# The mLSTM key sums of one head taken tile by tile over batches 1 to 3

## The chip, the cores and the metric

The kernel runs on 1 core of one Trainium2 chip. The metric is the device time of one execution in microseconds (us). The kernel before takes 1183.11 us, the median of 3 runs (1175.84 to 1189.69).

## The reference, cut to what matters

The program is one inference step of two layers. Layer 0 mixes a gated recurrence with dilated attention; layer 1 is an mLSTM block with 4 heads of 512 dimensions. A prompt of 256 tokens and 8 sample sequences of 4 tokens each go through together, and all of it is in float32. The change touches the mLSTM block alone, and there the running sum of the keys, `n`:

```python
w_state = jnp.exp(bcum[:, -1:, :] - bcum + ic - m_new[:, None, :])
decay = jnp.exp(bcum[:, -1] + m - m_new)
kw = kc * w_state[..., None]
C_new = decay[..., None, None] * C + jnp.einsum('bshd,bshe->bhde', kw, vc)
n_new = decay[..., None] * n + jnp.sum(kw, axis=1)
```

For each head and each sequence there is a state matrix `C` (512 by 512) and a vector `n` (512). `C` gets the sum over tokens of outer products of weighted keys and values; `n` gets the sum over tokens of the weighted keys. The new `n` is only an output: nothing later in the step reads it. `C` before the update is read by the queries of the samples. The 8 samples bring their `C` from HBM and write it back (8 MB in and 8 MB out in every head's turn); the prompt starts from zero and writes its own.

## The kernel before, in words

Every engine has its own instruction stream, written out by hand, and semaphores order them. The dense projections multiply 128x128 weight tiles by 288 token columns in three products (high by high, low by high, high by low; lines 1964 to 1966). Between the projection into the mLSTM block and the one out of it lies the **state stage**, which is what matters here. It loops over 4 heads `h`, and in each over the 8 samples `b`, which the code calls batches.

In batch `b` TensorE does `old_state(h, b)` (the samples' queries times the old `C`, L2419, 4 products that use 32 columns of the array each) and `outer(h, b, 0)` and `outer(h, b, 1)` (the outer products of that sample, L2446, each half of `C` into two PSUM banks: banks 0 and 1, or 4 and 5, by turns). The prompt's own outer products are items of the same kind, `outer(h, NB, 0)` ahead of batch 3's and `outer(h, NB, 1)` ahead of batch 4's (L2449, 4 products of 512 columns). Each of them may begin when the item that last used its two banks has been taken out: VectorE does that for a sample (`new_state`, L1687, decay times old `C` plus the banks, into the ring `cring`), ScalarE for the prompt (`prompt_state`, L1090). SyncE stores each item when it is made (L637) and, when the store of an earlier item has freed a slot of the ring of ten, loads the item that comes eight later (L628). All of the stage's large transfers are on this one queue.

Other work of a head hangs on the batches. After batch 0 TensorE makes denominators and numerators of the prompt (L2375 to L2392). VectorE scales them into `hT` (L1751) and ScalarE squares `hT` (L1106). In batch 2 TensorE sums the squares over the rows, `row_squares` (L2457, 4 products of 256 columns against ones), ScalarE takes the root (L1108), VectorE the reciprocal (L1759) and two passes over `hT` (L1761 in batch 2, L1769 in batch 3). In batches 4 to 7 TensorE makes queries, keys and values of the next head.

The **key sums** are `key_sums`: for each of the 4 tiles `e` of a head's 512 dimensions, products of one column (the prompt's weighted keys, L2403) and one of eight columns (the samples', L2405), all into one PSUM bank. Before, they run in batch 1, two tiles ahead of `outer(h, 1, 0)` and two between it and `outer(h, 1, 1)`. VectorE's `new_n` (L1675 to L1678) turns them into the new `n` at the end of its batch 1.

Two PSUM banks, 6 and 7, are **staging banks**. Their users stand in the list `USES`, in the order of a head; use number `u` gets bank 6 + u % 2. Before TensorE writes use `u` it waits until use `u - 2`, the last one in that bank, has been read. `DVE_READS` names the uses that VectorE reads; `n` is one, `mean` (the row squares) is read by ScalarE. Every use counts up `stage_full` once, and its reader waits for its own number, so the order of the list must be the order in which TensorE finishes them.

Of the kernel before, what the change touches and what calls it, by code (L numbers as in the profile page):

```python
# [25 lines left out]
P = 128  # L26
D = 1024
SEQ = 256
NB = 8
# [21 lines left out]
NH = 4  # L51
DH = DC // NH
ET = DH // P
# [55 lines left out]
assert ITEMS % 2 == 0  # L109

USES = ["q0", "q1", "q2", "q3", "k0", "k1", "k2", "k3", "kt0", "kt1", "ks", "vt0", "vt1", "vs",
        "bc0", "bc1", "sc", "n", "mean"]
VT_BANKS = (6, 7, 2, 3, 6, 7)
AB_USES = (["qs", "q0", "ks", "k0"] + [f"r{m}" for m in range(4)] + [f"i{m}" for m in range(4)]
           + [f"r{m}" for m in range(4, 8)] + [f"i{m}" for m in range(4, 8)])
# [25 lines left out]
def program(nc, A, O):  # L141
    ctx = ExitStack()
    with ctx:
# [5 lines left out]
        def at(name, off, *dims, dt=F32, parts=P):  # L149

            off = (off + 31) // 32 * 32
            n = int(np.prod(dims))
            assert off + 4 * n <= ARENA, (name, off + 4 * n - ARENA)
            t = nc.alloc_sbuf_tensor_at(name, [parts, n], dt, offset=arena0 + off)[:, :]
            if len(dims) == 2:
                t = t.rearrange("p (a b) -> p a b", b=dims[1])
            if len(dims) == 3:
                t = t.rearrange("p (a b c) -> p a b c", b=dims[1], c=dims[2])
            return t, (off + 4 * n + 31) // 32 * 32
# [108 lines left out]
        seln, o = at("seln", o, NB, dt=F32R, parts=3 * NS)  # L268
        gsml, o = at("gsml", o, 2 + NB, parts=NH)
        tokg, o = at("tokg", o, 2, 2 * NH)  # L270
# [25 lines left out]
        ktok, o = at("ktok", o, 2, DH)  # L296
# [20 lines left out]
        kst, o = at("kst", o, 2, DH, dt=F32R, parts=3 * NS)  # L317
# [4 lines left out]
        ps = ctx.enter_context(nc.psum_tensor("ps", [P, 8, 512], F32))  # L322
# [179 lines left out]
        def use(h, name):  # L502

            return len(USES) * h + USES.index(name)
# [664 lines left out]
        def _(dve):  # L1169
# [574 lines left out]
            def chunk(h, b):  # L1744
                if b == 0:

                    dve.wait_ge(den_abs, h + 1)
                    order.after(dve.tensor_tensor(dn, dn, bc[:, h % 2, R_EN:R_EN + SEQ], ALU.max))
                    order.after(dve.reciprocal(dn, dn))
                    dve.wait_ge(num_psum, h + 1)  # L1750
                    dve.tensor_tensor(hT, ps[:, 4:6, :].rearrange("p a (c t) -> p (a c) t", t=SEQ),  # L1751
                                      dn.unsqueeze(1).to_broadcast([P, ET, SEQ]), ALU.mult).then_inc(h_ready, 1)
                    if h == 2:
                        sample_stats(0)
                if b == 1:
                    new_n(h)
                if b == 2:
                    dve.wait_ge(stage_read_a, reads(use(h, "mean"))[1])
                    order.after(dve.reciprocal(dn, dn))  # L1759
                    for e in range(ET):  # L1760
                        order.mark(dve.scalar_tensor_tensor(hT[:, e], hT[:, e], pcol("norm_w", ET * h + e), dn,  # L1761
                                                            ALU.mult, ALU.mult))
                    if h + 1 == NH:
                        dve_lo(0, 0, STEP0[OUT_C])
                if b == 3:
                    order.wait()
                    for e in range(ET):
                        m = ET * h + e
                        order.mark(dve.scalar_tensor_tensor(hT[:, e], xcc[:, m, 0:SEQ], pcol("skip", m), hT[:, e],  # L1769
                                                            ALU.mult, ALU.add))  # L1770
                    order.wait()
                    dve.wait_ge(z_ready, h + 1)
                    dve.tensor_tensor(hT, hT, z[:, ET * h:ET * h + ET, 0:SEQ], ALU.mult).then_inc(y1_full, 1)
                    if h >= 2:
                        sample_folds(h - 2)
                    if h == 2:
                        sample_gates(0)
                        sample_scales(0)
                    if h + 1 == NH:
                        dve_lo(1, 0, STEP0[OUT_C])  # L1780
                if b == 5 and h == 2:
                    sample_rows(0)
                if b == 5 and h + 1 < NH:
                    keys_low(h + 1)
                if b == 6 and h + 1 < NH:
                    values_low(h + 1)
                if b == 7 and h == 2:
                    sample_low(0)
                if b == (7 if h + 1 < NH else 4):
                    dve.wait_ge(y1_hi_ready, h + 1)  # L1790
                    dve.tensor_tensor(y1_lo[:, ET * h:ET * h + ET, 0:SEQ], hT, y1_hi[:, ET * h:ET * h + ET, 0:SEQ],
                                      ALU.subtract).then_inc(y1_ready, 1)
                if b == 7:
                    if h + 1 < NH:
                        queries(h + 1)
                        arguments(h + 1)
                        weights(h + 1)
# [153 lines left out]
        def _(pe):  # L1951
# [252 lines left out]
            for h in range(H):  # L2204
# [21 lines left out]
                for i in range(3):  # L2226
                    last = pe.transpose(ps[:, 6, P * i:P * i + P], pS[f][:, P * i:P * i + P], ident)
# [8 lines left out]
                out = ps[:, 7, SEQ * f:SEQ * f + SEQ]  # L2236
# [65 lines left out]
            def staged(h, name):  # L2302

                u = use(h, name)
                if u >= 2:
                    pe.wait_ge(*reads(u - 2))
                return ps[:, 6 + u % 2]
# [85 lines left out]
                                     skip_group_check=True)  # L2393
                last.then_inc(num_psum, 1)

            def key_sums(h, tiles):

                out = staged(h, "n") if 0 in tiles else ps[:, 6 + use(h, "n") % 2]
                for e in tiles:
                    c0 = (NB + 2) * e  # L2400
                    es = slice(P * e, P * e + P)
                    for tt in range(2):
                        pe.matmul(out[:, c0 + NB:c0 + NB + 1], ktok[:, tt, es], tokg[:, tt, NH + h:NH + h + 1],  # L2403
                                  start=tt == 0, stop=tt == 1)
                    last = pe.matmul(out[:, c0:c0 + NB], kst[:, h % 2, es], seln, start=True, stop=True)  # L2405
                if ET - 1 in tiles:
                    last.then_inc(stage_full, 1)

            def old_state(h, b):
# [98 lines left out]
            for h in range(NH):  # L2508
                for b in range(NB):
                    last = old_state(h, b)  # L2510
                    if b == NB - 1:
                        last.then_inc(hs_psum, 1)
                    if b == 1:
                        key_sums(h, (0, 1))
                    if b == 2:
                        row_squares(h)
                    if b in (3, 4):
                        outer(h, NB, b - 3)
                    outer(h, b, 0)
                    if b == 1:  # L2520
                        key_sums(h, (2, 3))
                    if h + 1 == NH and b + 1 == NB:
                        sum_groups(h)
                    outer(h, b, 1)
                    chunk(h, b)
# [145 lines left out]
```

## Time and profile before

| | us |
|---|---|
| median of 3 runs | 1183.11 |
| lowest and highest run | 1175.84, 1189.69 |
| the profiled execution, its device time | 1187.85 |
| the profiled execution, its span | 1185.9 |
| mean granted TensorE clock over the span | 0.966 |

All rows below are of this one profiled execution. Times in them are in microseconds from the start of its span. "Busy" of TensorE (PE) is the time in which a matmul is under way, whatever it does; PEld is its weight loads, which overlap. PEclk is the clock that TensorE was granted, as a share of its full 2.4 GHz; it has two levels, 1.00 and 0.50 (1.2 GHz), and a mean between them is a stretch with some of each. In a row of the timeline the first number is the start, the second the time from that start to the end of the group's last instruction; neighbouring matmuls overlap, so the time that a group takes from the engine is read from its start to the start of the next. Brackets at the end of a row give idle time ahead of it and what ended it.

### The profile page before, as it was taken

What the parts mean: (1) busy time and instruction counts of PE and PEld (TensorE: products, weight loads), DVE (VectorE), ACT (ScalarE), POOL (GpSimd) and SP (SyncE); (2) the same over time, 40 slices, a digit from 0 to 9 for tenths busy, and PEclk for the clock granted to TensorE, in tenths of its full rate; (3) what the DMA queues carried; (4) which work ended last, traced back from release to release, by engine and by line L of the source; (5) the groups of instructions that cost most, each with busy time, mean ns of one, the idle gap of its engine ahead of it and who ended that gap; (6) DMA issues with size and microseconds to landing.
All of it is one profiled execution on the core that took longest, in us unless ns stands there. A gap on an engine that the chain in (4) does not pass through costs nothing.

```text
span 1185.9 us, 21692 instructions
## 1 busy us (share of the span) xinstructions
PE 1101.5 (93%) x8497; PEld 962.3 (81%) x8497; DVE 660.9 (56%) x958; ACT 542.9 (46%) x884; POOL 150.4 (13%) x204
## 2 busy tenths in 40 slices
PE   4998998777999999999999999999998999999996
PEld 4986877656999999999899965656555999999995
DVE  4568674412456444343997636666768366544343
ACT  5332635212555554344475353645543366553431
POOL 5133000000002221001400220100000003220000
PEclk9998999788999999999999999898989999999998
DMA  9696897799334544454644039898989634554441
GB/s 339 220 345 251 309 347 283 264 327 381 129 122 148 169 163 160 164 172 160 232 143 143 19 107 337 318 358 282 386 298 404 215 107 165 169 167 160 163 140 40
DMA packets 92265, 260.97 MB, mean 220 GB/s; under 512 B 8837, under 2 KB 9861, under 8 KB 91801
## 3 DMA queue, kind: packets, MB, share of 16 engines
q1 hardware_dynamic: 91320, 257.92, 61.2%
q0 software_dynamic: 432, 1.29, 0.4%
q8 instruction: 56, 0.92, 0.3%
q10 hardware_dynamic: 432, 0.65, 0.2%
q14 instruction: 25, 0.20, 0.1%
HBM read 218.10 MB, written 41.73 MB: 219 GB/s over the span
## 4 chain that ended last, share of the span: by engine, by line
PE 80%; DVE 11%; ACT 4%; DMA 2%; issue 2%; POOL 0%; SPq 0%; POOLq 0%; ACTq 0%; DVEq 0%
PE ps L1964 19%; PE ps L1966 19%; PE ps L1965 19%; PE ps L2419 2%; PE ps L2446 2%; PE ps L2076 2%; DVE w_lo L1175 2%; PE ps L2157 2%; PE ps L2317 2%; PE ps L2449 1%; DMA kv_b<-in_kv 1%; PE ps L2457 1%; DVE rstd L1202 1%; PE ps L2324 1%; DVE cring L1687 1%
## 5 line engine op out<-in xcount | busy, mean ns | idle before, releaser
L1175 DVE TENSOR_TENSOR w_lo<-w_raw,w_hi 128x1024 fp32r<-128x1024 f32 x232 | 284.6, 1233 | 205.0 <-ACT w_hi L692 204.0
L692 ACT ACTIVATE w_hi<-w_raw 128x1024 fp32r<-128x1024 f32 x232 | 242.0, 1053 | 196.2 <-PE ps L1966 182.1
L1964 PE MATMUL ps<-xin_hi,w_hi 128*128 128x288 f32 x1016 | 308.3, 303 | 24.8 <-DVE w_lo L1175 23.7
L1965 PE MATMUL ps<-xin_lo,w_hi 128*128 128x288 f32 x1016 | 304.7, 300 | 0.0
L1966 PE MATMUL ps<-xin_hi,w_lo 128*128 128x288 f32 x1016 | 304.4, 300 | 0.0
L1964 PEld LDWEIGHTS ps<-xin_hi,w_hi 128*128 128x128 f32 x1016 | 194.8, 192 | 37.7 <-DVE w_lo L1175 21.1
L1965 PEld LDWEIGHTS ps<-xin_lo,w_hi 128*128 128x128 f32 x1016 | 194.3, 191 | 0.7 <-issue 0.2
L1966 PEld LDWEIGHTS ps<-xin_hi,w_lo 128*128 128x128 f32 x1016 | 193.8, 191 | 0.0
L1966 PE MATMUL ps<-hid_hi,w_lo 128*128 128x288 f32 x512 | 151.9, 297 | 0.0
L1965 PE MATMUL ps<-hid_lo,w_hi 128*128 128x288 f32 x512 | 151.4, 296 | 0.0
L1964 PE MATMUL ps<-hid_hi,w_hi 128*128 128x288 f32 x512 | 151.2, 295 | 0.0
L1687 DVE SCALAR_TENSOR_TENSOR cring<-cring,bc,ps 128x1024 f32<-128x1024 f32 x64 | 79.5, 1276 | 43.9 <-PE ps L2446 43.4
L1964 PEld LDWEIGHTS ps<-hid_hi,w_hi 128*128 128x128 f32 x512 | 96.7, 189 | 0.0
L1965 PEld LDWEIGHTS ps<-hid_lo,w_hi 128*128 128x128 f32 x512 | 96.3, 188 | 0.0
L1966 PEld LDWEIGHTS ps<-hid_hi,w_lo 128*128 128x128 f32 x512 | 96.1, 188 | 0.0
L1848 POOL TENSOR_TENSOR hid_lo<-relu,hid_hi 128x288 f32 x64 | 52.5, 820 | 181.5 <-ACT hid_hi L766 181.5
L1267 DVE SCALAR_TENSOR_TENSOR relu<-ps,rstd 128x288 f32<-128x288 f32 x64 | 29.1, 457 | 78.9 <-PE ps L1966 75.5
L764 ACT ACTIVATE relu<-relu 128x288 f32<-128x288 f32 x64 | 28.4, 443 | 69.9 <-DVE relu L1267 68.5
L1838 POOL COPY sqsum<-sq 128x288 f32<-128x288 f32 x5 | 3.1, 612 | 438.3 <-ACT sq L752 433.4
L2446 PE MATMUL ps<-vb,kst 96*128 96x512 f32 x128 | 46.4, 465 | 8.8 <-ACT cring L1090 5.2
L2446 PEld LDWEIGHTS ps<-vb,kst 96*128 96x128 f32 x128 | 22.5, 198 | 33.4 <-issue 14.7
L752 ACT ACTIVATE sq<-ps 128x288 f32<-128x288 f32 x32 | 13.2, 411 | 75.6 <-PE ps L1966 75.6
(398 smaller groups left out, 1710.8 us busy)
## 6 DMA issues: line engine op xcount, KB each, us to landing
w_raw<-in_weights SPq DMA_DIRECT2D x232, 512.0 KB, 3.3
cring<-in_C SPq DMA_DIRECT2D x64, 512.0 KB, 6.3
out_Cs<-cring SPq DMA_DIRECT2D x64, 512.0 KB, 6.2
kv_a<-in_kv SPq DMA_DIRECT2D x60, 448.0 KB, 5.7
kv_b<-in_kv SPq DMA_DIRECT2D x60, 448.0 KB, 5.8
out_Cp<-cring SPq DMA_DIRECT2D x8, 512.0 KB, 5.4
kv_w<-in_kv SPq DMA_DIRECT2D x8, 448.0 KB, 5.1
x<-in_x SPq DMA_DIRECT2D x1, 1152.0 KB, 7.5
```

What stands on the lines that cost most here:

```text
L692: act.activation(w_hi[:, l % UM], w_raw[:, l % W_SLOTS], ACT.Copy).then_inc(hi_ready, 1)
L764: act.activation(relu2[:, l % 2], relu[:, l % 2], ACT.Square).then_inc(relu2_ready, 1)
L1175: dve.tensor_tensor(w_lo[:, l % W_SLOTS], w_raw[:, l % W_SLOTS], w_hi[:, l % UM], ALU.subtract).then_inc(lo_ready, 1)
L1267: dve.scalar_tensor_tensor(relu[:, l % 2], ps[:, bank, 0:T], 0.0, rstd, ALU.max, ALU.mult).then_inc(out_taken, 1)
L1687: dve.scalar_tensor_tensor(cring[s], cring[s], bc[:, h % 2, R_DECAY + b:R_DECAY + b + 1], new, ALU.mult, ALU.add).then_inc(c_new, 1)
L1848: pool.tensor_tensor(hid_lo[:, bass.ds(m, 1)].rearrange("p a t -> p (a t)"), relu2[:, l], hid_hi[:, bass.ds(m, 1)].rearrange("p a t -> p ( ...
L1964: pe.matmul(out, w_hi[:, j, ws], hi, start=start and kk == 0, stop=False)
L1965: pe.matmul(out, w_hi[:, j, ws], lo, start=False, stop=False)
L1966: last = pe.matmul(out, w_lo[:, l % W_SLOTS, ws], hi, start=False, stop=stop and kk == UK - 1)
L2076: last = pe.matmul(ps[32 * b4:32 * b4 + 32, 4 + c, 0:NK // 2], qz_of[b4][:, h], kv[s][:, c * NK // 2:(c + 1) * NK // 2], start=h == 0, sto ...
L2157: last = pe.matmul(out, pT[:, kt, c0:c0 + 32], kv[s][:, P * kt:P * kt + P], start=kt == 0 and h % 4 == 0, stop=False, skip_group_check=True)
L2446: last = pe.matmul(out, kst[:, h % 2, es], vb[:, (NB * h + b) % 2], start=True, stop=True)
```

## The change

The key sums are taken one tile at a time: tile 0 ahead of `outer(h, 1, 0)` as before, tiles 1, 2 and 3 each between the two outer products of batches 1, 2 and 3. `row_squares`, in batch 2, now comes before the last two tiles, so `mean` changes places with `n` in `USES`. VectorE's `new_n` goes from batch 1 to batch 3, where it stands ahead of the pass L1769. The number and the shapes of all instructions stay as they are.

```diff
@@ -109,7 +109,7 @@
 USES = ["q0", "q1", "q2", "q3", "k0", "k1", "k2", "k3", "kt0", "kt1", "ks", "vt0", "vt1", "vs",
-        "bc0", "bc1", "sc", "n", "mean"]
+        "bc0", "bc1", "sc", "mean", "n"]
@@ -1752,7 +1752,7 @@
-                if b == 1:
+                if b == 3:
                     new_n(h)
                 if b == 2:
                     dve.wait_ge(stage_read_a, reads(use(h, "mean"))[1])
@@ -2393,17 +2393,16 @@
-            def key_sums(h, tiles):
-
-                out = staged(h, "n") if 0 in tiles else ps[:, 6 + use(h, "n") % 2]
-                for e in tiles:
-                    c0 = (NB + 2) * e
-                    es = slice(P * e, P * e + P)
-                    for tt in range(2):
-                        pe.matmul(out[:, c0 + NB:c0 + NB + 1], ktok[:, tt, es], tokg[:, tt, NH + h:NH + h + 1],
-                                  start=tt == 0, stop=tt == 1)
-                    last = pe.matmul(out[:, c0:c0 + NB], kst[:, h % 2, es], seln, start=True, stop=True)
-                if ET - 1 in tiles:
+            def key_sums(h, e):
+
+                out = ps[:, 6 + use(h, "n") % 2] if e else staged(h, "n")
+                c0 = (NB + 2) * e
+                es = slice(P * e, P * e + P)
+                for tt in range(2):
+                    pe.matmul(out[:, c0 + NB:c0 + NB + 1], ktok[:, tt, es], tokg[:, tt, NH + h:NH + h + 1],
+                              start=tt == 0, stop=tt == 1)
+                last = pe.matmul(out[:, c0:c0 + NB], kst[:, h % 2, es], seln, start=True, stop=True)
+                if e == ET - 1:
                     last.then_inc(stage_full, 1)
@@ -2511,14 +2510,14 @@
                     if b == 1:
-                        key_sums(h, (0, 1))
+                        key_sums(h, 0)
                     if b == 2:
                         row_squares(h)
                     if b in (3, 4):
                         outer(h, NB, b - 3)
                     outer(h, b, 0)
-                    if b == 1:
-                        key_sums(h, (2, 3))
+                    if 1 <= b < ET:
+                        key_sums(h, b)
                     if h + 1 == NH and b + 1 == NB:
                         sum_groups(h)
                     outer(h, b, 1)
```

## Rows read from the trace of the kernel before

**Rows 1.** The page: busy time of TensorE over the span, and its granted clock in 40 slices.

```profile
PE 1101.5 (93%) x8497; PEld 962.3 (81%) x8497; DVE 660.9 (56%) x958; ACT 542.9 (46%) x884; POOL 150.4 (13%) x204
PEclk9998999788999999999999999898989999999998
```

**Rows 2.** Busy time by stretch: the last head's turn in the state stage.

```profile
core 0: us, PE busy (x) PEld busy (x) DVE busy (x) ACT busy (x) POOL busy (x), PEclk, DMA share, GB/s
862.00:912.00 50.00, 45.58 (x235) 25.00 (x234) 38.02 (x58) 19.46 (x30) 0.00 (x0) 0.93 0.94 340
```

**Rows 3.** Busy time by stretch around the fall of the clock, heads 0, 1, 3; last, batch 5 of head 3.

```profile
709.00:713.00 4.00, 4.00 (x32) 2.91 (x24) 2.46 (x2) 1.06 (x1) 0.00 (x0) 1.00 0.55 207
713.40:716.70 3.30, 3.30 (x12) 1.50 (x5) 1.48 (x4) 1.90 (x2) 0.00 (x0) 0.50 0.87 225
764.60:771.30 6.70, 6.70 (x22) 3.77 (x21) 2.22 (x5) 2.00 (x2) 0.00 (x0) 0.50 0.74 256
873.90:880.50 6.60, 6.60 (x21) 3.66 (x20) 2.07 (x5) 2.00 (x2) 0.00 (x0) 0.50 0.78 239
896.00:899.00 3.00, 1.34 (x5) 0.60 (x4) 3.00 (x3) 0.39 (x1) 0.00 (x0) 1.00 1.06 409
```

**Rows 4.** The timeline of TensorE in batches 1 to 3 of head 0.

```profile
start us, us, engine line op out<-in xcount [idle before <-releaser]
709.77 0.61 PE L2403 MATMUL ps<-tokg,ktok 128*128 128x1 f32 x4
...
710.91 0.71 PE L2446 MATMUL ps<-vb,kst 96*128 96x512 f32 x2
711.45 0.50 PE L2403 MATMUL ps<-tokg,ktok 128*128 128x1 f32 x4
...
712.49 0.71 PE L2446 MATMUL ps<-vb,kst 96*128 96x512 f32 x2
713.13 1.81 PE L2419 MATMUL ps<-cring,qz 128*32 128x512 f32 x8
714.86 2.90 PE L2457 MATMUL ps<-qf,ones 128*128 128x256 f32 x8
717.41 1.28 PE L2446 MATMUL ps<-vb,kst 96*128 96x512 f32 x4
718.62 1.07 PE L2419 MATMUL ps<-cring,qz 128*32 128x512 f32 x8
719.62 3.70 PE L2449 MATMUL ps<-vw,ktok 128*128 128x512 f32 x8
722.75 1.03 PE L2446 MATMUL ps<-vb,kst 96*128 96x512 f32 x2
724.43 0.73 PE L2446 MATMUL ps<-vb,kst 96*128 96x512 f32 x2 [0.65 <-ACT cring L1090]
```

**Rows 5.** The timeline of TensorE in head 1, from the second outer product of batch 1.

```profile
764.94 1.20 PE L2446 MATMUL ps<-vb,kst 96*128 96x512 f32 x2
766.07 1.94 PE L2419 MATMUL ps<-cring,qz 128*32 128x512 f32 x8
767.94 3.66 PE L2457 MATMUL ps<-qf,ones 128*128 128x256 f32 x8
771.16 1.12 PE L2446 MATMUL ps<-vb,kst 96*128 96x512 f32 x3
```

**Rows 6.** The timeline of ScalarE, head 0: the prompt's first item taken out.

```profile
723.35 1.02 ACT L1090 ACTIVATE cring<-ps 128x1024 f32<-128x1024 f32 x1 [5.08 <-PE ps L2449]
```

**Rows 7.** The timeline of VectorE: `new_n` of head 0, then batch 2 of head 3.

```profile
714.43 0.16 DVE L1675 COPY pack_n<-ps 128x4 f32<-128x4 f32 x1
...
714.72 0.19 DVE L1678 TENSOR_TENSOR pack_n<-pack_n,ps 128x32 f32<-128x32 f32 x1
...
881.24 2.47 DVE L1687 SCALAR_TENSOR_TENSOR cring<-cring,bc,ps 128x1024 f32<-128x1024 f32 x2 [4.31 <-PE ps L2446]
```

**Rows 8.** The timeline of TensorE in head 3: batch 4 begins; batch 5 waits for VectorE.

```profile
888.07 1.06 PE L2419 MATMUL ps<-cring,qz 128*32 128x512 f32 x8
...
897.20 0.73 PE L2446 MATMUL ps<-vb,kst 96*128 96x512 f32 x2 [1.20 <-DVE cring L1687]
```

**Rows 9.** SyncE's queue in head 3, and the page's row on such loads (KB each, median us to landing).

```profile
876.98 0.47 SPq L628 DMA_DIRECT2D cring<-in_C  x1
...
cring<-in_C SPq DMA_DIRECT2D x64, 512.0 KB, 6.3
```

## The prediction

> **What bounds the kernel now.** I read the page first. TensorE is busy for 93% of the span, and its granted clock is a little under full in many slices [rows 1]: time goes either where TensorE is idle or where it runs at half clock. The busy time by stretch for each head's turn comes next. In the last turn TensorE is busy for 45.58 of 50 us, the clock averages 0.93 and the DMA engines are busy for 94% at 340 GB/s [rows 2]; the other three turns are alike, with a busier TensorE. So the state stage has two near bounds, TensorE and the transfers of `C`, and a clock that is not full although TensorE has hardly a pause.
>
> Finer stretches show where. In head 0 the clock is 1.00 up to 713 us and 0.50 from about 713.3 to 716.7; in heads 1 and 3 it is 0.50 for 6.7 and 6.6 us, and head 2 is like them. Each head has just one such stretch, with TensorE busy throughout [rows 3]. The timeline says what the engine did before each fall: it had just gone through the key sums of batch 1 [rows 4]. They take 1.14 us for two tiles (709.77 to 710.91) and 1.04 for the other two (711.45 to 712.49), 2.18 us in all for 8 products of one column and 4 of eight columns: busy by the profile, with hardly anything streamed. Right behind them stand the two blocks that pay at half clock, `old_state` of batch 2 and the row squares.
>
> **The change, part by part.** The sum goes against the profiled execution's own 1187.85 us.
>
> *Row squares.* At half clock they take 2.55 us in head 0 (714.86 to 717.41, partly at full clock) [rows 4] and 3.22 in head 1 (767.94 to 771.16) [rows 5]; heads 2 and 3 repeat head 1. The full-clock price comes from the prompt's outer products, 8 instructions of 512 float32 columns in 3.13 us (719.62 to 722.75) [rows 4]: half the columns, 1.57 us. If the clock stays full this is worth 0.98 + 3 x 1.65 = 5.9 us.
>
> *`old_state` of batch 2.* It takes 1.73 us in head 0 (713.13 to 714.86) against 1.00 in batch 3 (718.62 to 719.62) [rows 4], and 1.87 in head 1 (766.07 to 767.94) [rows 5]. Worth 0.73 + 3 x 0.87 = 3.3 us.
>
> *The second outer product of batch 1.* At half clock it takes 1.13 us in head 1 (764.94 to 766.07) [rows 5] against 0.64 in head 0 (712.49 to 713.13) [rows 4]; head 3 is like head 1. Worth 2 x 0.49 = 1.0 us. Other pieces (the start of a fall in a last key tile, eight small transposes of head 2) I take at nothing.
>
> So a clock that stays up would give 10.2 us. The bound from above is half of all half-clock time, (3.4 + 3 x 6.8) / 2 = 11.9 us, the lengths being those of [rows 3] with their unsampled edges. The bound from below is nothing gained, or something lost (a rival below). Why I take 10.2: after the change the longest run without a full block holds two tiles, not four. In order it is `old_state` 1.00, tile 0.55, outer 0.6, tile 0.55, outer 0.6, `old_state` 1.00, row squares 1.57; tiles 2 and 3 have 1.0 to 3 us of streaming on either side. And TensorE at 1.34 busy of 3.00 us in batch 5 of head 3, with waits for VectorE, keeps a clock of 1.00 [rows 3]: sparser than what the changed batches would be.
>
> By the Trainium skill, "TensorE: Matmul & The Clock Gate", section "HAM oscillation — how this bites in real kernels", the clock falls through idle gaps between bursts of matmuls, and a busy engine keeps it. By that rule the key sums, which leave no gap, would not be the cause and the clock part of the sum would be 0. The trace disagrees as it stands: 4.00 busy of 4.00 us before a fall, no fall at 1.34 of 3.00.
>
> *Tile 3.* In batch 3 it comes between `outer(h, 3, 0)` and `outer(h, 3, 1)`. There TensorE idles 0.65 us, until ScalarE has emptied the banks of the prompt's first item (1.02 us) [rows 4, 6]. A tile costs 2.18 / 4 = 0.55, so it fits in the wait: batch 1 is 0.55 shorter and batch 3 no longer, 4 x 0.55 = 2.2 us. If that cover were gone it would be 0. Tiles 1 and 2 cost the same in their places as before.
>
> *Tile 2* delays VectorE's use of `outer(h, 2, 1)`. VectorE is busy with `outer(h, 2, 0)` then: two uses take 2.47 us [rows 7], 1.24 each, and tile and outer product take 1.2. Nothing.
>
> *Row squares earlier by two tiles*, 1.1 us. They wait for ScalarE's squares, which were done more than 3 us before them in head 0. Nothing.
>
> *`new_n` in batch 3* is three instructions from 714.43 to 714.91 [rows 7], about 0.45 us. In batch 1 VectorE had room. In batch 3 it lies ahead of L1769, and in heads 2 and 3 VectorE's chain from batch 2 on sets the pace: in head 3 TensorE waits 1.20 us for it [rows 8]. Cost 0.45 us in each of those heads, but the chain starts earlier by tile 2 as well as tile 3, 0.55 more than counted. Net nothing. Its reader's release is needed by `q1` of the next head, behind batch 4's outer products, 5 us later: no wait.
>
> *Staging.* `mean` now takes the bank whose last use was `bc1`, and `n` the one of the scores; both were read before batch 0. The next head's `q0` waits for ScalarE's root instead of `new_n`, long past by then. No DMA is moved.
>
> *Transfers.* A shorter TensorE path asks for `C` sooner. The tightest load is that of batch 4's second half, issued at 876.98 and used from 888.07, 11.1 us for a landing of 6.3 [rows 8, 9]. After the change the issue is some 1.7 us earlier and the use 4: 8.7 us for 6.3. It still fits, with 2.4 to spare instead of 4.8.
>
> **Sum:** 10.2 + 2.2 = 12.4 us, 1187.85 to 1175.4. The profiled execution is 4.7 us above the median of the three. The same instructions got a stretch of 3.4 us in one head and 6.7 in another [rows 3], so the length of these stretches is not fixed by the program, and a run at the median has probably lost less to them. If the whole 4.7 came from them, the changed kernel would be at 1175.4; if none of it did, at 1170.7. I take a value nearer the first, 1174.5, which is 8.6 us (0.7%) under the median before.
>
> **The rivals.**
>
> *The clock falls as before* (also the case in which the page's rule holds). Against it: the fall comes behind the key sums in all four heads. For it: I know this from one execution, and stretches of half clock exist in earlier stages that have no key sums [rows 1]. Then tile 3 alone counts, 1183.11 - 2.2 = 1180.9 us.
>
> *Head 2 alone still falls*, since its eight small transposes follow `outer(2, 1, 1)`: it keeps about 2.5 of the 10.2 us, and the time is 1177. This lies within the forecast's own range.
>
> *The transfers become the bound.* The last turn has 340 GB/s over 50 us, and where nothing holds the queue it moves 409 [rows 2, 3]: 340 x 50 / 409 = 41.6 us is its floor, and a turn 4 us shorter is at 46. The bytes fit, but a load that lands 2.5 us later than the median holds batch 4. If that takes half of the clock's gain: 1174.5 + 5.1 = 1179.6.
>
> *Slower:* the clock falls twice in a head. Tiles 2 and 3 carry thin work into batches 2 and 3, and in batch 3 TensorE also has the rest of the wait for ScalarE, just ahead of batch 4's prompt products, the densest block of the head. It decides from the point at which the granted clock shows a second half-clock stretch per head. Its price is that of the present one, 10.2 us over the four heads, with tile 3's gain of 2.2 against it: 1183.11 + 8.0 = 1191. Against it speaks that a tile is now alone between blocks that stream.
>
> **How the numbers follow.** Forecast (with head 2's case) 0.60, clock as before 0.22, transfers 0.10, a second fall 0.08. Predicted 1174.5. The forecast's own range is 1167 to 1181: from 1170.7 to 1177, widened by the scatter of a median of runs that differ by 13.85 us. The second case spreads 1176 to 1186, so the range that leaves out 2 in 10 is 1166.5 to 1186. A change under 1% (11.8 us) can't be told from none here, so "faster" is under 1171.3: 0.42 of the forecast's cases, 0.25 in all, with 0.01 from the others, 0.26. Slower than 1194.9 needs the second fall and a slow draw, 0.04, and 0.01 for what I have not thought of: 0.05. The rest, 0.69, is within 1%.
>
> **What would show each step.** No half-clock stretch between batches 1 and 2 of any head; row squares at 1.6 us from start to next start, `old_state` of batch 2 at 1.0; no idle time of TensorE ahead of `outer(h, 3, 1)`, or under 0.2 us; each head's turn shorter by 2.2 to 4 us; `new_n` right behind batch 3's two `new_state`. The prediction is wrong if the clock falls behind the row squares or in batch 3 instead, if `old_state` of batch 4 waits for a load, or if the 12 us of the stage are there and the stages behind it take longer.

## The result, and the profile after

The changed kernel takes 1176.38 us, the median of 20 executions (1170.96 to 1182.03); 20 of the kernel before have a median of 1182.0 (1174.35 to 1190.01). The ratio is 0.995, with a 95% interval of 0.9928 to 0.9972. Timed again later (9 executions), it is 0.9928 (0.9891 to 0.9966). Ratios and their intervals leave out an execution that took over 1.5% more than the fastest of its kernel; there was one (tile 3 alone moved, 1190.76 us). The forecast was 1174.5 in a range of 1166.5 to 1186: a small gain, and it came.

The profiled execution took 1179.63 us, 8.2 less than that of before (1187.85). Its page has the same busy TensorE as [rows 1], and a clock line that has lost its eights in the state stage.

```profile
PE 1096.1 (93%) x8497; PEld 961.2 (82%) x8497; DVE 661.2 (56%) x958; ACT 542.8 (46%) x884; POOL 150.0 (13%) x204
...
PEclk9998999978899999999999999999999999999998
```

Take the busy time by stretch at the places of [rows 3]. The first four rows are batches 1 to 3 of head 0, and batch 2 of heads 1, 2 and 3 (less exactly placed); the last two are the only half-clock stretches of this stage.

```profile
core 0: us, PE busy (x) PEld busy (x) DVE busy (x) ACT busy (x) POOL busy (x), PEclk, DMA share, GB/s
710.00:714.00 4.00, 4.00 (x31) 2.07 (x30) 2.94 (x3) 1.70 (x2) 0.00 (x0) 1.00 0.55 208
714.00:718.00 4.00, 4.00 (x25) 2.91 (x25) 2.07 (x3) 1.83 (x3) 0.00 (x0) 1.00 0.78 233
764.00:768.00 4.00, 4.00 (x25) 2.92 (x25) 2.05 (x3) 1.88 (x3) 0.00 (x0) 1.00 0.78 228
814.00:818.00 4.00, 4.00 (x25) 2.75 (x17) 1.46 (x2) 2.06 (x4) 0.00 (x0) 1.00 0.83 223
867.00:871.00 4.00, 4.00 (x25) 2.76 (x17) 2.06 (x3) 3.15 (x4) 0.00 (x0) 1.00 0.71 157
850.90:854.30 3.40, 3.40 (x7) 1.54 (x6) 3.33 (x14) 2.10 (x6) 0.00 (x0) 0.51 1.07 413
888.50:891.90 3.40, 3.40 (x12) 1.20 (x12) 3.07 (x4) 0.72 (x1) 0.00 (x0) 0.50 1.05 406
```

The clock is 1.00 in batches 1 to 3 of all four heads. It fell in two new places instead, for 3.4 us each: in batch 7 of head 2, and in batch 6 of head 3. The second of these stands right behind batch 5 of head 3, where TensorE waits for VectorE again and again:

```profile
885.00:888.50 3.50, 1.61 (x8) 0.59 (x4) 3.50 (x4) 0.60 (x1) 0.00 (x0) 1.00 1.05 406
```

The prediction had read the same kind of piece, 1.34 busy of 3.00 us at a clock of 1.00 [rows 3], as a sign that sparse work is safe. Here the clock is 1.00 for as long as the sparse piece lasts, and falls at its end.

The timeline of TensorE in head 0 answers to [rows 4]:

```profile
710.95 0.61 PE L2402 MATMUL ps<-tokg,ktok 128*128 128x1 f32 x4
...
711.53 0.71 PE L2445 MATMUL ps<-vb,kst 96*128 96x512 f32 x2
712.08 0.50 PE L2402 MATMUL ps<-tokg,ktok 128*128 128x1 f32 x4
...
712.56 0.70 PE L2445 MATMUL ps<-vb,kst 96*128 96x512 f32 x2
713.19 1.06 PE L2418 MATMUL ps<-cring,qz 128*32 128x512 f32 x8
714.18 1.99 PE L2456 MATMUL ps<-qf,ones 128*128 128x256 f32 x8
715.83 0.81 PE L2445 MATMUL ps<-vb,kst 96*128 96x512 f32 x2
...
721.73 1.03 PE L2445 MATMUL ps<-vb,kst 96*128 96x512 f32 x2
722.59 0.50 PE L2402 MATMUL ps<-tokg,ktok 128*128 128x1 f32 x4
722.96 0.25 PE L2404 MATMUL ps<-seln,kst 96*128 96x8 f32 x1
723.40 0.73 PE L2445 MATMUL ps<-vb,kst 96*128 96x512 f32 x2 [0.20 <-ACT cring L1090]
```

The row squares take 1.65 us (714.18 to 715.83) where they took 2.55, `old_state` of batch 2 takes 0.99 where it took 1.73. Tile 3 lies between the outer products of batch 3, and from the first of these to the second there are 1.67 us (721.73 to 723.40), as there were 1.68 before without the tile: it is free.

VectorE in the same head, against [rows 7]: `new_n` now stands behind the two updates of batch 3, and L1769 follows.

```profile
722.79 2.67 DVE L1687 SCALAR_TENSOR_TENSOR cring<-cring,bc,ps 128x1024 f32<-128x1024 f32 x2 [0.27 <-PE ps L2445]
725.37 0.16 DVE L1675 COPY pack_n<-ps 128x4 f32<-128x4 f32 x1
...
725.77 1.67 DVE L1769 SCALAR_TENSOR_TENSOR hT<-xcc,par,hT 128x256 f32<-128x256 f32 x4
```

**Where the 8.2 us lie.** I measure a turn of a head from its first denominator product to that of the next head, and that of head 3 to the first product of the output projection; the stage runs from the first outer product (702.63 before, 703.81 after) to the same end (906.69 and 896.37). Each number is a difference of two starts of the timeline.

| us | head 0 | head 1 | head 2 | head 3 | stage |
|---|---|---|---|---|---|
| before | 52.29 | 53.78 | 55.37 | 41.62 | 204.06 |
| after | 50.08 | 50.00 | 53.53 | 37.95 | 192.56 |
| difference | 2.21 | 3.78 | 1.84 | 3.67 | 11.50 |

What lies ahead of the stage was 1.2 us longer and what lies behind it 2.1 us longer (281.3 against 279.2, with a half-clock stretch at 984 us that the other execution had not): 11.5 - 1.2 - 2.1 = 8.2.

### The profile page after: what moved, and what is told of

The parts are those of the page before. It is cut to its first block, busy times and chain, and to the rows that moved or that the text cites. A ratio compares the mean times of both kernels' runs of the same rounds, so it can differ in the third digit from the quotient of the medians.

```text
span 1177.7 us, 21692 instructions
## 1 busy us (share of the span) xinstructions
PE 1096.1 (93%) x8497; PEld 961.2 (82%) x8497; DVE 661.2 (56%) x958; ACT 542.8 (46%) x884; POOL 150.0 (13%) x204
## 4 chain that ended last, share of the span: by engine, by line
PE 80%; DVE 10%; ACT 4%; DMA 3%; issue 2%; POOL 0%; SPq 0%; POOLq 0%; DVEq 0%; ACTq 0%
PE ps L1964 19%; PE ps L1966 19%; PE ps L1965 19%; PE ps L2445 2%; PE ps L2418 2%; PE ps L2076 2%; DVE w_lo L1175 2%; PE ps L2157 2%; PE ps L2317 2%; PE ps L2448 2%; DMA kv_b<-in_kv 1%; DVE rstd L1202 1%; PE ps L2324 1%; PE ps L2058 1%; PE ps L2361 1%
## 5 line engine op out<-in xcount | busy, mean ns | idle before, releaser
L1841 POOL TENSOR_TENSOR sqsum<-sqsum,sq 128x288 f32<-128x288 f32 x31 | 25.0, 808 | 162.1 <-ACT sq L752 161.1
```

Of the source, the lines that this page charges most:

```text
L1841: pool.tensor_tensor(sqsum, sqsum, sq[:, m % 2], ALU.add).then_inc(sq_added, 1)
```

## The experiments

The ratio is that of executions of the kernel named to those of before on the same chip, with its 95% interval; it can differ by 0.002 from the quotient of the two medians. Before had 1180.75 (23 executions) beside the block and the first wide kernel, 1179.77 (32) beside tile 3 alone, tile 3 uncovered, the stage begun later and the first kernel with tiles in batches 1 to 4, and 1181.62 (18) beside the last three timed. The columns of the turns are from one profile each.

| kernel | median us (n) | ratio | head 0, 1, 2, 3 | stage |
|---|---|---|---|---|
| before, 2nd profile | 1184.26 (1) | | 52.29, 53.79, 55.37, 41.64 | 204.10 |
| before, 3rd profile | 1178.07 (1) | | 52.28, 52.12, 52.20, 40.12 | 197.72 |
| change, 2nd profile | 1176.96 (1) | | 50.07, 49.99, 54.77, 39.33 | 195.17 |
| change, timed again | 1174.09 (9) | 0.9928 (0.9891 to 0.9966) | 50.08, 50.00, 52.03, 40.00 | 193.11 |
| four tiles in one block | 1182.89 (12) | 0.9996 (0.9969 to 1.0023) | 50.63, 50.88, 52.17, 39.39 | 194.08 |
| wide tiles, order of before | 1176.52 (12) | 0.9957 (0.9933 to 0.9981) | 50.65, 50.55, 52.21, 39.49 | 193.94 |
| tile 3 alone moved | 1179.70 (12) | 0.998 (0.9949 to 1.001) | 51.71, 49.99, 55.17, 40.78 | 198.65 |
| tile 3 uncovered | 1177.55 (12) | 0.9974 (0.9944 to 1.0003) | 50.64, 50.55, 53.80, 37.69 | 193.68 |
| stage begun later | 1186.65 (12) | 1.0052 (1.0019 to 1.0085) | 52.25, 53.79, 55.35, 41.62 | 204.05 |
| tiles in batches 1 to 4 | 1171.84 (9) | 0.9924 (0.9896 to 0.9952) | 49.68, 49.61, 51.81, 37.33 | 189.46 |
| the same, again | 1168.85 (6) | 0.9875 (0.9837 to 0.9912) | 49.68, 49.59, 51.81, 39.64 | 191.76 |
| the same, wide tiles | 1171.53 (10) | 0.9912 (0.9879 to 0.9944) | 49.68, 49.60, 51.83, 37.25 | 189.37 |

### Both kernels once more, and before a third time

No edit.

> The kernel before, unchanged, to see a second execution of its state stage. Stage length is taken from the first outer product of head 0 to the first product of the output projection; it was 204.1 us in the profile before and 192.6 in the profile after. Theory A (half-clock stretches are a matter of where in an execution the key sums happen to fall): at least one of the four stretches behind the key sums is missing or has another length, and the stage is shorter by about half of the half-clock time that is missing. Rival B (the key sums always bring the clock down): four stretches again, 204 us within 1.

> The changed kernel, unchanged, to see a second execution. Theory A: no half-clock stretch between batches 1 and 3 of any head; the stage is at most 192.6 us, and about 189 if the two stretches that the first profile had elsewhere in it (3.4 us each, between heads 2 and 3 and in batch 6 of head 3) are absent. Rival B (the clean batches 1 to 3 were luck): one or more stretches there, row squares at up to 3.2 us.

> The kernel before, a third profile. Its first two had the same four half-clock stretches and a stage of 204.1 us, while its runs differ by up to 17 us. Theory A (executions near the median or under it have fewer or shorter stretches there): if this execution takes under 1180 us, at least one stretch is missing or shorter and the stage is under 202 us. Rival B (the stage is always 204 us and the scatter comes from elsewhere): 204.1 within 1 whatever the time.

The second profile of before repeats the first to 0.1 us, four stretches included: my theory lost that one. The third goes the other way, and at a time under the median as theory A has it. The clock fell in heads 0 and 1 for 3.4 us each and, late in the stage, for 6.8; in heads 2 and 3 it did not fall behind the key sums. Here is TensorE in head 0 and then head 2 of that third profile, the same instructions in the same order:

```profile
707.82 1.40 PE L2419 MATMUL ps<-cring,qz 128*32 128x512 f32 x8
709.15 3.30 PE L2457 MATMUL ps<-qf,ones 128*128 128x256 f32 x8
712.10 1.28 PE L2446 MATMUL ps<-vb,kst 96*128 96x512 f32 x4
...
812.18 0.68 PE L2467 MATMUL ps<-ident,hs 32*128 32x32 f32 x8
812.79 1.06 PE L2419 MATMUL ps<-cring,qz 128*32 128x512 f32 x8
813.78 1.99 PE L2457 MATMUL ps<-qf,ones 128*128 128x256 f32 x8
815.42 1.29 PE L2446 MATMUL ps<-vb,kst 96*128 96x512 f32 x4
```

Row squares: 2.95 us in head 0, 1.64 in head 2, and a stage that is 6.3 us shorter than in the first profile. What before loses to the clock differs by the execution. The change's second profile had full clock in heads 0 and 1 (50.07, 49.99), half-clock stretches of 3.4 us twice in head 2's turn, one of them over its row squares (2.39 us), and one of 6.8 us in the last batches of head 3. The first of these is the case "head 2 alone" of the prediction, in one profile of three. The Trainium skill, "TensorE: Matmul & The Clock Gate", section "What's actually happening", says of the rise of the clock that its moment differs from run to run of one kernel. These traces say of the fall that even whether it comes differs.

### Four tiles in one block

```diff
-                        key_sums(h, (0, 1))
+                        key_sums(h, (0, 1, 2, 3))
...
-                    if b == 1:
-                        key_sums(h, (2, 3))
```

> The order of before, but all four key tiles in one piece of 2.2 us ahead of the first outer product of batch 1. Theory A (a piece of thin work brings the clock down, the longer the likelier): the clock falls behind it in at least three heads, row squares at 2.5 to 3.2 us; time as before or up to 4 us slower, ratio 1.000 to 1.004. Rival B (what matters is that the row squares or old_state stand right behind the key sums): two outer products now stand between, the clock falls less often, ratio 0.995. Rival C (the clock has nothing to do with the key sums): same as before.

In the profile the clock stayed full from head 0 to head 2, with the four tiles in 2.26 us (709.07 to 711.33) and TensorE otherwise as before:

```profile
709.07 0.61 PE L2403 MATMUL ps<-tokg,ktok 128*128 128x1 f32 x4
...
711.33 1.16 PE L2446 MATMUL ps<-vb,kst 96*128 96x512 f32 x4
712.42 1.06 PE L2419 MATMUL ps<-cring,qz 128*32 128x512 f32 x8
713.41 1.99 PE L2457 MATMUL ps<-qf,ones 128*128 128x256 f32 x8
715.05 1.28 PE L2446 MATMUL ps<-vb,kst 96*128 96x512 f32 x4
```

Theory A named at least three falls, and there was none behind the key sums in that profile (one of 3.4 us came in batch 6 of head 3): a miss. But this execution took 1177.68 us, the fourth fastest of the twelve, and the ratio of all is 0.9996, which lies next to A's figure (and C's, which falls with the next kernel) and not B's 0.995. TensorE also waited twice for a load of `C`, 0.26 us in head 1 and 0.70 in head 3, as in no profile of before or of the change. One profile shows what a stage costs at a given clock; how often the clock falls can only be read from many executions.

### Wide tiles in the order of before

```diff
-                    c0 = (NB + 2) * e
+                    c0 = P * e
...
-                        pe.matmul(out[:, c0 + NB:c0 + NB + 1], ktok[:, tt, es], tokg[:, tt, NH + h:NH + h + 1],
+                        pe.matmul(out[:, c0 + NB:c0 + P - NB], ktok[:, tt, es],
+                                  tokg[:, tt, NH + h:NH + h + 1].to_broadcast([P, P - 2 * NB]),
```

> The order of before; the prompt's product of each key tile streams the same column 112 times over instead of once (two instructions as before, only wider), so a tile does not get shorter, and may get up to 0.1 us longer. Theory A (the clock falls because the key sums stream next to nothing): no half-clock stretch in batches 1 to 3 of any head, row squares at 1.65 us; the time against before is the change's without what tile 3 gives: ratio 0.996 to 0.999 with tiles that cost the same. Rival B (it is the number of small instructions, or the position of the block, not what is streamed): stretches as before, ratio 1.000 to 1.002.

This is the experiment that separates position from content. Each product of the prompt's keys streams 112 equal columns instead of one; everything stands where it stood before, and `new_n` reads the sums at their new columns.

```profile
711.23 0.70 PE L2403 MATMUL ps<-tokg,ktok 128*128 128x112 f32 x4
...
711.81 0.68 PE L2403 MATMUL ps<-tokg,ktok 128*128 128x112 f32 x4
...
712.37 0.71 PE L2447 MATMUL ps<-vb,kst 96*128 96x512 f32 x2
```

Two tiles take 1.14 us (711.23 to 712.37), exactly as in [rows 4]: the 111 extra columns are free. And the clock around them stays up:

```profile
711.00:714.60 3.60, 3.60 (x29) 2.92 (x25) 1.92 (x2) 1.06 (x1) 0.00 (x0) 1.00 0.36 135
714.60:718.00 3.40, 3.40 (x20) 2.26 (x20) 1.64 (x4) 2.38 (x3) 0.00 (x0) 1.00 0.79 197
```

Row squares are 1.64 us in all heads, and over 12 executions the ratio is 0.9957, nearly the change's; that is just under A's 0.996 to 0.999 and well away from B's 1.000 to 1.002. The mean granted clock of these executions is 0.9758, against 0.9724 over 73 executions of before. By the Trainium skill, "TensorE: Matmul & The Clock Gate", section "HAM oscillation — how this bites in real kernels", a busy engine keeps its clock. By that rule width could not matter here, since TensorE is busy throughout either way, for 4.00 of 4.00 us before a fall [rows 3] and for 3.60 of 3.60 here; the difference of 0.0034 in the mean clock (interval 0.0014 to 0.0053) says that it does. Nor is it a matter of the moment (see "The stage begun later"), for the wide tiles take the same time and move nothing ahead of a fall.

### Tile 3 alone, and tile 3 without its cover

In the first, batch 1 keeps tiles 0 and 1 ahead of its first outer product and tile 2 behind it, and only tile 3 goes to batch 3 (against the changed kernel):

```diff
                     if b == 1:
                         key_sums(h, 0)
+                        key_sums(h, 1)
...
-                    if 1 <= b < ET:
-                        key_sums(h, b)
+                    if b in (1, 3):
+                        key_sums(h, 2 if b == 1 else 3)
```

In the second, the change is kept, but tile 3 stands ahead of the prompt's item:

```diff
+                    if b == 3:
+                        key_sums(h, 3)
                     if b in (3, 4):
                         outer(h, NB, b - 3)
...
-                    if 1 <= b < ET:
+                    if 1 <= b < ET - 1:
                         key_sums(h, b)
```

> Only tile 3 moves to batch 3, between the two outer products; tiles 0 and 1 ahead of batch 1's first outer product and tile 2 between them stay as before. new_n in batch 3 and the staging order as in the change. Theory A (the change gains 2.2 us by tile 3 under ScalarE's wait in every execution, and a clock part that differs from one execution to the next): idle time of TensorE ahead of outer(h,3,1) falls from 0.65 to 0.20 us as in the change, ratio to before 0.996 to 0.999, somewhat worse than the change's 0.995 since 1.65 us of thin work stay together. Rival (spreading all four tiles is what counts): ratio 0.999 to 1.000 and half-clock stretches of batches 1 and 2 as before.

> The change with tile 3 ahead of the prompt's first item of batch 3 and not between the two outer products behind it: the thin work is as spread as in the change, but no wait covers this tile. Theory A: TensorE idles 0.65 us ahead of outer(h,3,1) again, and each turn is 0.5 us longer than the change's where the clock is the same: 50.6 us for a turn at full clock against 50.0; median about 2 us over the change's, ratio to before 0.996 to 0.998. Rival (the tile's place does not matter, the clock is all): turns of 50.0 us, ratio 0.995.

Uncovered, TensorE idles 0.64 us ahead of the second outer product of batch 3 again:

```profile
715.39 3.68 PE L2448 MATMUL ps<-vw,ktok 128*128 128x512 f32 x8
718.51 1.03 PE L2445 MATMUL ps<-vb,kst 96*128 96x512 f32 x2
720.18 0.73 PE L2445 MATMUL ps<-vb,kst 96*128 96x512 f32 x2 [0.64 <-ACT cring L1090]
```

Its turns at full clock are 50.64 and 50.55 us, the change's 50.08 and 50.00: the cover is worth 0.55 us a head, 2.2 in all, as forecast. With tile 3 alone moved, head 1 has the change's 49.99 where the clock stays up, and heads 0, 2 and 3 have row squares at 2.69, 2.83 and 2.83 us. The two theories' ratios for it, 0.996 to 0.999 and 0.999 to 1.000, can't be told apart by 0.998 (0.9949 to 1.001): inconclusive but for the turns.

### The stage begun later

```diff
+                if h == 0 and b == 0:
+                    for _ in range(2):
+                        pe.matmul(ps[:, 2, :], ones, ktok[:, 0], start=True, stop=True, skip_group_check=True)
```

> The order of before, with two more dense products (512 columns each, 1.6 us together) ahead of the state stage: the same stage, begun 1.6 us later on TensorE. The two profiles of before had the same four half-clock stretches, at 10.7, 61.9, 116.5 and 171.1 us from the stage's start. Theory A (whether the clock falls depends on where in time the key sums come, not on their order alone): stretches missing or of other length than those, stage length without the addition other than 204.1 by 2 us or more. Rival (the order alone decides): the same four stretches, stage 204.1 us from its first outer product, whole execution 1.6 us longer than before, ratio 1.001.

The added products took 1.91 us, of which 0.88 filled a wait that stood behind them in before, so the stage began about 1.0 us later. The profile is that of rival B: the same four stretches and 204.05 us. The times are not: 1186.65 us against 1179.77 for before on the same chip, ratio 1.0052 (6.1 us), for a delay of 1.0 us, and the mean granted clock of the 12 executions is 0.9689 against 0.9724. At the same clock (by a line through the executions of before, which comes below) these executions are only 1.0 us over before, the delay itself. So with the order unchanged, the later moment, or the two products themselves, changes how much half clock the executions get; the run can't tell these two apart. The profile by itself does not show it.

### A step further

```diff
-                if b == 3:
-                    new_n(h)
...
-                    for half in range(2):
-                        new_state(h, b, half)
+                    new_state(h, b, 0)
+                    if b == 4:
+                        new_n(h)
+                    new_state(h, b, 1)
...
-                    if b == 1:
-                        key_sums(h, 0)
...
-                    if 1 <= b < ET:
-                        key_sums(h, b)
+                    if 1 <= b <= ET:
+                        key_sums(h, b - 1)
```

> A step on: tiles 0 to 3 each between the outer products of batches 1 to 4, new_n between VectorE's two state updates of batch 4. The wait for ScalarE ahead of outer(h,4,1), 0.65 us in both kernels, covers another tile. Theory A: idle there 0.2 us, each turn 0.5 us shorter than the change's at the same clock (49.5 us for a turn at full clock), median about 2 us under the change's, ratio to before 0.992 to 0.995. Rival (new_n now holds up VectorE and the next head's first staging uses): turns of 50.0 us or more, ratio 0.995 to 0.998.

> The order with tiles in batches 1 to 4 once more, beside the changed kernel on the same chip. Theory A: 2 to 4 us under the changed kernel, of which 2 us (4 tiles of 0.5) come from the second covered wait and the rest from the clock; idle ahead of outer(h,4,1) 0.2 us. Rival (its first result was scatter of the chip): within 1 us of the changed kernel.

> The changed kernel again, timed beside the next two on the same chip, and a third profile of it. Theory A: ratio to before 0.995 within 0.003; in the profile head 0 and head 1 at 50.0 us a turn with row squares of 1.64 us. Rival (its first two profiles were lucky draws): half-clock row squares in two or more heads.

The wait ahead of the second outer product of batch 4, 0.65 us in before and in the change, now covers a tile too:

```profile
726.40 1.03 PE L2445 MATMUL ps<-vb,kst 96*128 96x512 f32 x2
727.26 0.50 PE L2402 MATMUL ps<-tokg,ktok 128*128 128x1 f32 x4
727.62 0.25 PE L2404 MATMUL ps<-seln,kst 96*128 96x8 f32 x1
728.08 0.73 PE L2445 MATMUL ps<-vb,kst 96*128 96x512 f32 x2 [0.20 <-ACT cring L1090]
```

A turn at full clock is 49.6 to 49.7 us, 0.4 under the change's and not 0.5: the view of the waits (us in total, times, longest) has new ones, of the next head's queries for `new_n`, and one for a load of `C`.

```profile
PEld ps L2317 <- DVE pack_n L1678: 1.6, 3, 0.9
...
PE ps L2317 <- DVE pack_n L1678: 0.5, 1, 0.5
...
PE ps L2418 <- DMA cring<-in_C: 0.2, 1, 0.2
```

This order beats before, and has the lower median beside the change: 1168.85 us beside the change's 1174.09 on the same chip, ratios to before of 0.9875 and 0.9928, and 0.9924 in its first session. The 5.2 us between the two medians are more than the 1.6 to 2 of the second cover, but they rest on 6 and 9 executions, and the intervals of the two ratios overlap (0.9837 to 0.9912, 0.9891 to 0.9966): how much the change is beaten by is not settled. The mean clock of this order is 0.9784 over its 15 executions, against the change's 0.9741 over 29.

The last kernel has this order with the products widened as in the wide kernel, and laid out in the bank as there:

```diff
-                    pe.matmul(out[:, c0 + NB:c0 + NB + 1], ktok[:, tt, es], tokg[:, tt, NH + h:NH + h + 1],
+                    pe.matmul(out[:, c0 + NB:c0 + P - NB], ktok[:, tt, es],
+                              tokg[:, tt, NH + h:NH + h + 1].to_broadcast([P, P - 2 * NB]),
```

> The order with a tile between the outer products of each of batches 1 to 4, and the prompt's products streaming the same column 112 times (at the same time per tile, 1.14 us for two tiles in the first wide kernel). Theory A (thin work brings the clock down, spread out it does so rarely, wide it does not): turns as in that order at full clock, 49.6 us, and hardly any gain from the width, since spreading has done it: ratio to that order 0.998 to 1.000, to before 0.991 to 0.993. Rival (spreading removes only a part, most falls of the stage come from its thin tiles in any order): another 2 us or more, ratio to before under 0.991.

It takes 1171.53, ratio 0.9912 (0.9879 to 0.9944): no further gain beside the narrow form's 0.9875 and 0.9924, as theory A had it. Neither the two profiles of the narrow form nor that of the wide one have half clock behind a key sum, so width has nothing left to gain there.

## Why the prediction was right, and where the expected 12 us went

**What bounds the stage**: right. TensorE at a reduced clock. **Row squares** at full clock: forecast 1.57 us, measured 1.64 or 1.65 in all heads of the profiled execution; **`old_state`** 1.00, measured 1.00; the **second outer product of batch 1** 0.64, measured 0.63 (712.56 to 713.19). **Tile 3**: forecast 0.55 us a head under the wait, measured 0.55. For the profiled pair the sum was 12.4 us and the stage gave 11.5; heads 0, 1 and 3, forecast at 2.3, 3.6 and 3.6, gave 2.21, 3.78 and 3.67. Head 2 gave 1.84, because the clock fell in its batch 7, where no key sums are: the scores take 3.76 us from start to next start there (852.40 to 856.16), 2.82 in before.

```profile
852.40 3.83 PE L2361 MATMUL ps<-qf,kf 128*128 128x256 f32 x16
856.16 0.41 PE L2364 MATMUL ps<-qf,kf 128*32 128x32 f32 x7
```

**The costs taken at nothing** held. `new_n` delays L1769 by 0.4 us in head 3 (from the first update of batch 3 to L1769: 2.38 us before, 2.78 after), and that turn still gained 3.67. No wait on staging appeared. **Transfers**: the load of batch 4's second half in head 3 was issued at 869.06 and used at 877.68, 8.6 us (forecast 8.7), against [rows 8, 9]; no wait for it.

```profile
869.06 0.54 SPq L628 DMA_DIRECT2D cring<-in_C  x1
...
877.68 1.06 PE L2418 MATMUL ps<-cring,qz 128*32 128x512 f32 x8
```

**What was only half right is the clock term, 10.2 us.** It is the price between an execution in which the clock falls in every head and one in which it falls in none. The text allowed for that by way of the median, and set the gain at 8.6 us; it was 5.6 (7.5 in the second session). The 1174.5 was picked between 1170.7 and 1175.4 by a guess at how much of the profile's 4.7 us above the median belonged to the clock; that it lies within 2 us of 1176.38 is in part luck. The term was too large for two reasons that the runs show. First, before does not always pay it: its stage was 204.06, 204.10 and 197.72 us in three profiles. Second, the changed kernel does not pay nothing: 192.56, 195.17 and 193.11 us, with 6.8 to 13.7 us at half clock in each, two thirds of it in the last batches of head 3. The means of the stage differ by 8.3 us over these six, and of that 2.2 are tile 3.

The granted clock in the traces of the same six profiles says how little of the gain is left over the whole span. In the mean, half clock in the stage went from 20.5 to 10.2 us; ahead of the stage, where nothing was changed, it went from 39.8 to 43.2, and behind it from 10.1 to 12.3. The total fell from 70.4 to 65.8 us only. What lies ahead of the stage can only be scatter; whether some of what lies behind it is half clock that the change has moved, three profiles of each can't say.

**The step of the prediction that did not hold** is the argument from batch 5 of head 3: sparser work had kept a clock of 1.00 there, so the changed batches would be safe, and nothing was put into the sum for a fall elsewhere. The changed batches were safe, but for head 2 in one profile. Batch 5 itself was not: in all three profiles of the change, and in one of the three of before, the clock fell at or behind its waits for VectorE, for 3.4 to 10.2 us. Heads 0, 1 and 3 gained what the sum gave them even so, since a fall of 3.4 us there costs next to nothing (below); the second profile has 6.8 us of it and a turn of 39.33, the third 10.2 us and 40.00, against 37.95.

Over all timed executions the mean clock went from 0.9724 (73) to 0.9741 (29), and the mean time from 1181.0 to 1175.5 us. Fitted by a line against its clock, before costs 11.1 us more for each 0.01 less, and at the same 0.973 the two kernels are at 1180.3 and 1176.5. So of 5.5 us only about 1.7 go with the mean clock (its rise of 0.0018 has a 95% interval, by drawing the executions anew, of 0.0001 to 0.0035, or 0.1 to 3.9 us by that line), and 3.8 do not. The line of before says what the 3.8 are. At the clocks that they had, the kernels in which a wait covers tile 3 are 3.6 us (the change) and 3.1 (tile 3 alone moved) under that line; those without a cover are 0.7 (uncovered) and 0.5 (wide) under it, and one block is within 0.2 us of it. Between the change and the uncovered kernel that is 2.9 us, interval 1.7 to 4.2, with the 2.2 of the turns inside it. So tile 3 accounts for the part that does not go with the clock, as far as these timings can tell.

What half clock costs in the last batches of head 3 depends on its length. With tiles in batches 1 to 4, head 3 took 37.33 us without any, 37.25 with 3.4 us of it (wide) and 39.65 with 6.8 (the narrow kernel again): nothing, and then 2.3 us, a third of the stretch. The first two hardly differ, and VectorE, which TensorE waits for there, is busy for 6.51 of 7.00 us; in the third it is busy for 4.79 of 6.80 us while TensorE is busy for 6.70.

```profile
878.00:885.00 7.00, 6.19 (x25) 2.03 (x26) 6.51 (x6) 1.32 (x2) 0.00 (x0) 0.76 1.05 407
878.80:885.60 6.80, 6.70 (x16) 1.58 (x16) 4.79 (x4) 0.60 (x1) 0.00 (x0) 0.50 1.05 407
```

**The rivals.** That the clock falls as before is refuted by the profiles of the change. A second fall in a head came once, in head 2 of its second profile (two of 3.4 us, as much half clock as the one fall of before). Transfers did not hold the change; they gave 0.2 us of waiting in one of two profiles of the order with tiles in batches 1 to 4, and 1.0 us in the kernel with one block. For the falls behind the key sums, the rule by which only gaps matter (the Trainium skill, "TensorE: Matmul & The Clock Gate", section "HAM oscillation — how this bites in real kernels") does not hold: the wide tiles say so. The falls in the last batches of head 3 do stand at gaps, waits of up to 1.44 us in the change's three profiles, with TensorE busy for 1.61 of 3.50 us ahead of one; no run tested what brings them about.

**Open**: why one block of four tiles times like before (0.9996), with a full clock behind its key sums in the one profile taken; what decides in which executions of one program the clock falls; and what the falls in the last batches of head 3 come from. A lead for the last two is the stage begun later, where 1.0 us moved the mean clock by as much as the wide tiles did, the other way.

## What to carry to other kernels

Look at the granted clock around small products that come in a row: here TensorE was 100% busy by the profile and lost its clock all the same, and the blocks behind paid. Look at it behind waits too: a sparse piece at full clock does not say that the next block keeps it. Put such products one by one into waits that exist already, where they cost nothing, or widen them as far as their time allows. Before putting a price on a clock stretch, ask whether a second profile has it; its price belongs to an execution, not to the program.

## What the runs showed that I had not expected

Widening a product from 1 to 112 columns of float32 cost no time here: two tiles are 1.14 us either way. Profiles of one program come out equal to 0.1 us in a stage of 204 us and then 6.3 us shorter. And two added products that delay a stage by 1.0 us made the kernel 0.5% slower, six times the delay itself; all but 1.0 us of it went with the clock.
